# First stack of a two-stack kernel on one core: the norm factor moved from the rows to the projections, the transposes of x and y spread between the products

## The chip, the core and the metric

The kernel runs on one core of one Trainium2 chip. The metric is device time in microseconds, from the start of the program to its end; lower is better. All arithmetic is fp32 in and out; the products are made of fp32r pieces (below).

## The reference

A sequence of 256 rows of width 2048 goes through two stacks of two layers each. The change touches the first stack only. One of its layers is:

```python
h = rms_norm(x, norm_gain)                      # x * rsqrt(mean(x*x)+eps) * gain, per row
proj = jnp.einsum('bsd,de->bse', h, w_in)       # 2048 -> 10 segments of 2048
(da_q, da_k, da_v, da_z, sb_q, sb_k, sb_v, sb_z, gate_a, gate_b) = split_columns(proj)
...
q = rope(rms_norm(da_q..., qk_q_gain)); k = rope(rms_norm(da_k..., qk_k_gain))
oa = differential_attention(...);  ua = rms_norm(oa, subln_gain) * (1-lambda_init) * silu(da_z)
ub = stick_breaking_attention(sb_q, sb_k, sb_v) * silu(sb_z)
y = sigmoid(gate_a) * (ua @ w_branch_a) + sigmoid(gate_b) * (ub @ w_branch_b)
return x + y @ w_out
```

The second stack (convolution, windowed attention and a recurrent unit side by side) starts from the x that layer 1 of the first leaves.

## The kernel before, in words

**Products.** Every weight matrix is cut into *halves* of 128 x 1024 numbers (512 KB). SyncE loads them one after the other into a ring of four slots (`raw`, `RING = 4`). ScalarE rounds a half to `w_hi` (line 551), VectorE makes the rest `w_lo = raw - w_hi` (line 913), and with that the raw slot is free for the next load. TensorE multiplies each half with two stationary parts of the activations, `hT_hi` and `hT_lo`: `product` (lines 1431 to 1433) issues three matmuls of 128x512 for two row groups of two blocks of the half, so twelve matmuls for a half. Eight halves make a *unit* (512 output columns) in two banks of PSUM `acc`; units take turns between banks 0, 1 and 2, 3. ScalarE can only round half s when TensorE is through with half s-4 (`split_free`, `acc_ready`).

**A layer** of stack one has 52 units: 16 steps (8 heads of differential attention, "DA", then 8 of stick-breaking, "SB") of two units each, whose attention work is pushed in between the halves of the step that follows; 16 units of gates and branches (unit g0 = 32 onwards, groups j = 0 to 3 of four units); 4 units of output projection. Orders on all engines are written out by hand: `split(u, a, b)` on ScalarE and VectorE and `halves(u, stat, a, b)` on TensorE name the halves of unit u (numbers of 8 and more run on into the next unit) that are worked on before the next other piece. The layer loop is a hardware loop (`Fori`).

**Between stages.** TensorE needs activations with features on the partitions, so they are *turned* (transposed) by it, four transposes of 128x128 for two of the 16 feature chunks (a *group* f = 0 to 7) into PSUM `work[:, f % 4]`; ScalarE copies this to the hi part and VectorE makes the lo part. Three such places matter here:

- `layer_start` (TensorE line 1455): after all of x is loaded (layer 0), or after the last `add_x` (layer 1), ScalarE sums the squares of x (line 572), GpSimd raises the mean to the power -0.5 (line 383), VectorE scales the rows of x into `rows` (line 919), TensorE turns `rows` in 8 groups, ScalarE (580) and VectorE (935) fill `hT`. Only then does the first product of the layer start. The gain `kept[:, c]` is applied in 580 and 935.
- `turn_y` (TensorE line 1566): when the last branch unit is done, groups 0 to 5 are turned, then, after `branch(l, 3, 1)` on VectorE (lines 1038, 1041), groups 6 and 7; lines 673 and 1045 fill `hT` again, and the output projection starts.
- `add_x` (VectorE line 1052) adds each of the four output units to x.

A DA step starts on GpSimd with `rotate` (squares, norm and rotary part of q and k, lines 408 to 426), from the copy of the first unit (`evac_qk`, ScalarE line 594), and TensorE turns its result `QN` (line 1468) after the first half of the next step.

## Time and profile before

| | us |
|---|---|
| median of 3 runs (lowest, highest) | 3442.09 (3440.69, 3442.84) |
| the profiled execution: its own time | 3441.07 |
| its span in the trace | 3439.4 |
| TensorE busy | 3328.3 (97%) |
| VectorE, ScalarE, GpSimd busy | 1981.0, 1640.6, 502.1 |

Mean granted TensorE clock 0.987. The profile's span is 1.7 us shorter than the execution's own time, which in turn is 1.0 us under the median. Busy time of the pipelined matmuls overlaps, so a matmul's share of time is read from the distance between starts and not from its duration.

### The profile page before, as it was taken

The numbers are of one execution on the slowest core, as the hardware profiler recorded it, in microseconds if no ns is written. First come the engines' busy times: TensorE is split into PE (matmuls) and PEld (weight loads), VectorE is DVE, ScalarE is ACT, GpSimd is POOL, SyncE is SP. The second block draws the span as 40 slices with busy tenths as digits, with TensorE's granted clock in tenths as the row PEclk, the third lists the DMA queues.
The fourth block names the chain that finished last, engine by engine and source line by source line (L and its number), as shares of the span: only waits on it lengthen the run. The fifth ranks groups of instructions, "written<-read, shape, count | busy, mean of one in ns | idle before, by whom it ended". The sixth has DMA issues, their size and how long they took to land.

```text
span 3439.4 us, 49065 instructions
## 1 busy us (share of the span) xinstructions
PE 3328.3 (97%) x17528; PEld 2846.8 (83%) x17528; DVE 1981.0 (58%) x2194; ACT 1640.6 (48%) x2243; POOL 502.1 (15%) x426
## 2 busy tenths in 40 slices
PE   6999999999999989999999999999969999999998
PEld 5888888888888778888888888888769889898897
DVE  4667654545444456667544444444556775667765
ACT  4444455555444444454455554443434464544643
POOL 4444500000000015445300000000001000020000
PEclk9999999999999999999999999999989999999998
DMA  5455554455555445555545545555533334343342
GB/s 195 170 172 185 172 177 168 165 177 169 193 194 192 169 162 177 177 177 175 179 161 175 171 171 184 192 193 183 179 135 130 123 126 151 138 158 123 120 145 98
DMA packets 155021, 567.22 MB, mean 165 GB/s; under 512 B 17296, under 2 KB 17344, under 8 KB 154368
## 3 DMA queue, kind: packets, MB, share of 16 engines
q1 hardware_dynamic: 153216, 555.81, 47.3%
q0 software_dynamic: 1680, 9.67, 0.8%
q8 instruction: 86, 1.41, 0.2%
q14 instruction: 39, 0.32, 0.0%
HBM read 563.32 MB, written 2.10 MB: 164 GB/s over the span
## 4 chain that ended last, share of the span: by engine, by line
PE 94%; DVE 3%; ACT 1%; issue 1%; DMA 1%; POOL 0%; DVEq 0%; ACTq 0%; POOLq 0%
PE acc L1431 22%; PE acc L1433 22%; PE acc L1432 22%; PE acc L1642 6%; PE acc L1644 6%; PE acc L1643 6%; PE work L1468 1%; DVE w_lo L913 1%; PE work L1494 1%; PE work L1720 1%; PE work L1721 1%; PE work L1691 1%; PE work L1621 1%; PE work L1622 1%; PE work L1623 0%
## 5 line engine op out<-in xcount | busy, mean ns | idle before, releaser
L913 DVE TENSOR_TENSOR w_lo<-raw,w_hi 128x1024 fp32r<-128x1024 f32 x1056 | 1407.9, 1343 | 1200.1 <-ACT w_hi L551 929.5
L551 ACT ACTIVATE w_hi<-raw 128x1024 fp32r<-128x1024 f32 x832 | 876.5, 1059 | 980.4 <-PE acc L1433 977.0
L1431 PE MATMUL acc<-w_hi,hT_hi 128*128 128x512 f32 x2816 | 1115.4, 396 | 0.0
L1433 PE MATMUL acc<-w_hi,hT_lo 128*128 128x512 f32 x2816 | 1099.2, 390 | 0.0
L1432 PE MATMUL acc<-w_lo,hT_hi 128*128 128x512 f32 x2816 | 1097.2, 390 | 0.0
L1433 PEld LDWEIGHTS acc<-w_hi,hT_lo 128*128 128x128 f32 x2816 | 529.2, 188 | 113.0
L1432 PEld LDWEIGHTS acc<-w_lo,hT_hi 128*128 128x128 f32 x2816 | 530.3, 188 | 106.4
L1431 PEld LDWEIGHTS acc<-w_hi,hT_hi 128*128 128x128 f32 x2816 | 529.9, 188 | 105.1
L565 ACT ACTIVATE w_hi<-raw 128x1024 fp32r<-128x1024 f32 x224 | 236.1, 1056 | 396.0 <-PE acc L1644 382.8
L1642 PE MATMUL acc<-h_hi,w_hi 128*128 128x272 f32 x1152 | 344.7, 299 | 0.0
L1644 PE MATMUL acc<-h_hi,w_lo 128*128 128x272 f32 x1152 | 333.2, 289 | 0.0
L1643 PE MATMUL acc<-h_lo,w_hi 128*128 128x272 f32 x1152 | 331.5, 288 | 0.0
L1642 PEld LDWEIGHTS acc<-h_hi,w_hi 128*128 128x128 f32 x1152 | 216.8, 188 | 4.4 <-issue 2.4
L1643 PEld LDWEIGHTS acc<-h_lo,w_hi 128*128 128x128 f32 x1152 | 217.1, 188 | 1.5
L1644 PEld LDWEIGHTS acc<-h_hi,w_lo 128*128 128x128 f32 x1152 | 216.7, 188 | 0.0
L1642 PE MATMUL acc<-PJr,w_hi 128*128 128x272 f32 x512 | 150.7, 294 | 0.0
L1644 PE MATMUL acc<-PJr,w_lo 128*128 128x272 f32 x512 | 148.2, 289 | 0.0
L1643 PE MATMUL acc<-PJr,w_hi 128*128 128x272 f32 x512 | 147.4, 288 | 0.0
L377 POOL TENSOR_SCALAR ZG<-TZ 128x512 f32<-128x512 f32 x32 | 21.3, 664 | 718.6 <-ACT TZ L589 718.6
L319 DVE SCALAR_TENSOR_TENSOR PJ<-PJ,par 128x271 f32<-128x271 f32 (+14 forms) x240 | 106.6, 496 | 0.0
L1433 PE MATMUL acc<-w_hi,ubT_lo 128*128 128x512 f32 x256 | 99.6, 389 | 0.0
L1431 PE MATMUL acc<-w_hi,ubT_hi 128*128 128x512 f32 x256 | 99.6, 389 | 0.0
(314 smaller groups left out, 3598.9 us busy)
## 6 DMA issues: line engine op xcount, KB each, us to landing
raw<-weights SPq DMA_DIRECT2D x1056, 512.0 KB, 3.3
mat<-mats POOLq DMA_DIRECT2D x2, 1536.0 KB, 7.7
X<-x_in POOLq DMA_DIRECT2D x1, 2048.0 KB, 12.8
out<-out_rows SPq DMA_DIRECT2D x8, 256.0 KB, 2.3
par<-params POOLq DMA_DIRECT2D x2, 640.0 KB, 8.8
cst<-consts POOLq DMA_DIRECT2D x1, 872.0 KB, 5.8
cst<-consts POOLq DMA_DIRECT2D x1, 768.0 KB, 13.7
ropeC<-rope POOLq DMA_DIRECT2D x2, 256.0 KB, 8.8
```

The costliest lines, as they stand in the source:

```text
L319: return eng.scalar_tensor_tensor(o[:, j:TOK], x[:, 0:TOK - j], par2[:, w:w + 1], o[:, j:TOK], ALU.mult, ALU.add)
L551: act.activation(w_hi[:, slot, :], raw[:, slot, :], ACT.Copy).then_inc(hi_ready, 1)
L565: act.activation(w_hi[:, slot, :], raw[:, slot, :], ACT.Copy).then_inc(hi_ready, 1)
L913: dve.tensor_tensor(w_lo[:, s % RING, :], raw[:, s % RING, :], w_hi[:, s % RING, :], ALU.subtract)\
L1431: pe.matmul(o, stat[0][:, kc, token], hi, start=(kc == 0), stop=False)
L1432: pe.matmul(o, stat[0][:, kc, token], lo, start=False, stop=False)
L1433: ins = pe.matmul(o, stat[1][:, kc, token], hi, start=False, stop=(kc == KC - 1))
L1468: ins = pe.transpose(work[:, a // 2, o:o + P], src[:, t, a, :], ident)
L1494: pe.matmul(work[:, 2 + a, 0:384], cst[:, C_NEGTRI:C_NEGTRI + P], SM[:, a, :], start=False, stop=True, skip_group_check=True)
L1642: pe.matmul(o, hi, x_hi, start=(kc == 0), stop=False)
L1643: pe.matmul(o, hi, x_lo, start=False, stop=False)
L1644: ins = pe.matmul(o, lo, x_hi, start=False, stop=(kc == KC - 1))
```

## The change

1. **Norm factor.** x is no longer scaled before it is turned. `hT` holds x times gain, and the factor of each row (`rstdx`, or half of it for the gates' tanh) is the scale of the ScalarE copies that empty the projections: `evac_qk`, `evac_vz`, `evac_gate`. These become two instructions of 128x512 (one for each row group, since the scale is one number per partition) in place of one of 128x1024. The squares and the GpSimd chain move into the first step of the layer, before `evac_qk`.
2. **Layer 0.** x is loaded by SyncE in eight pieces of 256 columns (256 KB each, in runs of 1 KB), placed between the first four weight halves; the identity and the gains (`kept`, now of both layers) go with them. GpSimd's own loads wait until the eighth piece is there. TensorE turns groups 0 and 1, then a group after each of the first six halves.
3. **Layer 1.** x is turned during the output projection of layer 0: groups 0 to 5 within units 1 to 3, groups 6 and 7 after the second half of the new layer. The per-layer parameters are loaded when the last y is ready, not after the last `add_x`.
4. **y** is turned into `uaT`, which is no longer read then, in place of `hT`: groups 0 to 5 between halves 9 to 14 of the last branch unit pair, groups 6 and 7 after the first two halves of the output projection.
5. The layer loop is written out twice in place of a `Fori`, and some semaphores are merged.

```diff
         @block.sync
+            def x_part(f):
+                c = slice(256 * f, 256 * f + 256)
+                sp.dma_start(X[:, :, c], x_in[:, c].rearrange("(t p) n -> p t n", p=P)).then_inc(x_loaded[f], 16)
+            x_part(0)
+            sp.dma_start(cst[:, C_ID:C_ID + P], consts1[:, C_ID:C_ID + P]).then_inc(set_loaded, 16)
             for slot in range(RING):
                 sp.dma_start(raw[:, slot, :], weights[slot]).then_inc(raw_loaded[slot], 16)
+                if slot == 0:
+                    sp.dma_start(kept[:, :, :], kept1).then_inc(set_loaded, 16)
+                x_part(slot + 1)
+            for f in range(RING + 1, 8):
+                x_part(f)
...
         @block.scalar
             def layer_start(l):
-                act.wait_ge(x_loaded, 16)
-                act.wait_ge(x_added, 4 * l)
-                for t in range(NT):
-                    act.activation(rows[:, t, :], X[:, t, :], ACT.Square, accum_out=ssx[:, t:t + 1]).then_inc(x_ss, 1)
-                split(UNITS1 * l, 0, RING)
+                u = UNITS1 * l
+                if l == 0:
+                    act.wait_ge(set_loaded, 32)
+                    for f in range(8):
+                        split(u, f, f + 1)
+                        h_hi(l, f)
+                else:
+                    split(u, 0, 6)
+                    h_hi(l, 6)
+                    h_hi(l, 7)
+                    split(u, 6, 8)
+            def first_step(m):
+                split(u, 8, 10)
+                act.wait_ge(x_added, 4 * l)
+                for t in range(NT):
+                    act.activation(rows[:, t, :], X[:, t, :], ACT.Square, accum_out=ssx[:, t:t + 1]).then_inc(x_ss, 1)
+                split(u, 10, 12)
+                act.wait_ge(x_rstd, 2 * l + 2)
+                evac_qk(m)
+                split(u, 12, 14)
...
             def evac_qk(m):
-                act.activation(QK[...], acc[:, 0:2, :], ACT.Copy).then_inc(qk_evac, 1)
+                for t in range(NT):
+                    ins = act.activation(QK[:, t, :, :]..., acc[:, t, :], ACT.Copy, scale=rstdx[:, t:t + 1])
+                ins.then_inc(qk_evac, 1)
...
         @block.vector
             def layer_start(l):
-                dve.wait_ge(x_rstd, l + 1)
-                for t in range(NT):
-                    dve.tensor_scalar(rows[:, t, :], X[:, t, :], rstdx[:, t:t + 1], None, ALU.mult).then_inc(xn_ready, 1)
...
         @block.tensor
+            def turn_h(l, f):
+                if l:
+                    pe.wait_ge(x_added, 4 * (l - 1) + f // 2 + 1)
+                else:
+                    pe.wait_ge(x_loaded[f], 16)
+                if f >= 4:
+                    pe.wait_ge(hT_lo, 8 * l + (f - 3))
+                ... 4 transposes of X into work[:, f % 4] ...
+            def first_step(m):
+                if l == 0:
+                    pe.wait_ge(set_loaded, 32)
+                    turn_h(l, 0)
+                    turn_h(l, 1)
+                pe.wait_ge(qk_evac, m["n"])
+                for s in range(8):
+                    halves(u, hT, s, s + 1, (hT_lo, 8 * l))
+                    if l == 0 and s < 6:
+                        turn_h(l, s + 2)
+                    if l and s == 1:
+                        turn_h(l, 6)
+                        turn_h(l, 7)
...
                 pe.wait_ge(y_ready, 4 * l + 3)
+                halves(g0 + 14, ubT, 8, 9)
                 for f in range(6):
+                    halves(g0 + 14, ubT, 9 + f, 10 + f)
                     turn_y(l, f)
+                halves(g0 + 14, ubT, 15, 16)
+                halves(g0 + 16, uaT, 0, 2, out)
                 pe.wait_ge(y_ready, 4 * l + 4)
                 for f in (6, 7):
                     turn_y(l, f)
-                halves(g0 + 16, hT, 0, 8, (yT_lo, 8 * l))
...
+                for n in range(1, 4):
+                    halves(g0 + 16 + n - n % 2, uaT, 8 * (n % 2), 8 * (n % 2) + 2)
+                    for f in (2 * n - 2, 2 * n - 1):
+                        if l + 1 < DEPTH:
+                            turn_h(l + 1, f)
+                        halves(..., s, s + 1)
+                    halves(..., 8 * (n % 2) + 4, 8 * (n % 2) + 8)
```

Below is how this stands in the instruction order of TensorE at three places, with the semaphores that each instruction waits for. First the start of layer 0 before the change: all 32 transposes of `rows`, then the first half (its first three matmuls are shown).

```order
L1455 MATMUL work<-cst,rows 128x128 [waits xn_ready]
L1455 MATMUL work<-cst,rows 128x128 x15
...
L1455 MATMUL work<-cst,rows 128x128 [waits hT_lo]
L1455 MATMUL work<-cst,rows 128x128 x3
...
L1424 ISA [waits hT_lo,qk_evac]
L1431 MATMUL acc<-w_hi,hT_hi 128x512 [waits split_ready]
L1432 MATMUL acc<-w_lo,hT_hi 128x512
L1433 MATMUL acc<-w_hi,hT_lo 128x512
```

The same place with the change: eight transposes of `X`, the first half, and a group of four after it.

```order
L1532 MATMUL work<-cst,X 128x128 [waits x_loaded0,set_loaded]
L1532 MATMUL work<-cst,X 128x128 x3
L1532 MATMUL work<-cst,X 128x128 [waits x_loaded1]
L1532 MATMUL work<-cst,X 128x128 x3
L1506 MATMUL acc<-w_hi,hT_hi 128x512 [waits split_ready,hT_lo,qk_evac]
...
L1532 MATMUL work<-cst,X 128x128 [waits x_loaded2]
L1532 MATMUL work<-cst,X 128x128 x3
L1506 MATMUL acc<-w_hi,hT_hi 128x512 [waits split_ready,hT_lo]
```

The 24 transposes of groups 2 to 7 have moved from in front of the first half to places behind the first six halves. Next, the turning of y: before the change, behind the last half of the last branch unit (`ubT`), on TensorE.

```order
L1433 MATMUL acc<-w_hi,ubT_lo 128x512
...
L1566 MATMUL work<-cst,rows 128x128 [waits y_ready]
L1566 MATMUL work<-cst,rows 128x128 x15
...
L1566 MATMUL work<-cst,rows 128x128 [waits yT_lo,y_ready]
L1566 MATMUL work<-cst,rows 128x128 x3
...
L1431 MATMUL acc<-w_hi,hT_hi 128x512 [waits split_ready]
```

With the change, the rows around groups 5 to 7: group 5 stands between two halves of `ubT`, groups 6 and 7 behind two halves of the output projection (`uaT`).

```order
L1664 MATMUL work<-cst,rows 128x128 [waits yT_lo]
L1664 MATMUL work<-cst,rows 128x128 x3
L1506 MATMUL acc<-w_hi,ubT_hi 128x512 [waits split_ready]
...
L1508 MATMUL acc<-w_hi,uaT_lo 128x512
L1664 MATMUL work<-cst,rows 128x128 [waits yT_lo,y_ready]
L1664 MATMUL work<-cst,rows 128x128 x3
L1664 MATMUL work<-cst,rows 128x128 [waits yT_lo]
L1664 MATMUL work<-cst,rows 128x128 x3
L1506 MATMUL acc<-w_hi,uaT_hi 128x512 [waits split_ready,yT_lo]
```

What moved is the wait for the last y (`y_ready`): from between the transposes to behind two halves of the output projection. Last, TensorE at the start of layer 1 with the change (before, the rows there are those of the first block above, since the loop body is one).

```order
L1506 MATMUL acc<-w_hi,hT_hi 128x512 [waits split_ready,hT_lo,qk_evac]
...
L1508 MATMUL acc<-w_hi,hT_lo 128x512
L1532 MATMUL work<-cst,X 128x128 [waits hT_lo,x_added]
L1532 MATMUL work<-cst,X 128x128 x3
L1532 MATMUL work<-cst,X 128x128 [waits hT_lo,x_added]
L1532 MATMUL work<-cst,X 128x128 x3
L1506 MATMUL acc<-w_hi,hT_hi 128x512 [waits split_ready,hT_lo]
```

The layer's first two halves no longer stand behind any transpose; groups 6 and 7 follow them.

## Rows read from the trace of the kernel before

**Rows 1.** Waits of TensorE, longest first: us in total, times, longest.

```profile
PE work L1455 <- DVE rows L919: 33.3, 2, 24.3
...
PE work L1566 <- DVE rows L1041: 8.2, 2, 4.1
```

**Rows 2.** Timeline, layer 0's start, all engines: start, length, what, releaser.

```profile
0.87 1.82 SPq L352 DMA_DIRECT2D raw<-weights  x4
...
14.27 1.28 ACT L572 ACT_TABLE_LOAD   x1 [14.27 <-DMA X<-x_in]
15.57 1.91 ACT L572 ACTIVATE rows<-X 128x2048 f32<-128x2048 f32 x1
...
25.83 3.01 ACT L580 ACTIVATE hT_hi<-work,kept 128x256 fp32r<-128x256 f32 x8
...
30.54 6.34 DVE L935 SCALAR_TENSOR_TENSOR hT_lo<-work,kept,hT_hi 128x256 fp32r<-128x256 f32 x16
...
34.50 0.48 PE L1431 MATMUL acc<-w_hi,hT_hi 128*128 128x512 f32 x1
```

**Rows 3.** Timeline of TensorE around the turning of y, layer 0.

```profile
1162.09 3.27 PE L1566 MATMUL work<-cst,rows 128*128 128x128 f32 x24
1169.48 1.97 PE L1566 MATMUL work<-cst,rows 128*128 128x128 f32 x8 [4.12 <-DVE rows L1041]
1171.10 0.78 PE L1431 MATMUL acc<-w_hi,hT_hi 128*128 128x512 f32 x1
...
1174.50 0.39 PE L1433 MATMUL acc<-w_hi,hT_lo 128*128 128x512 f32 x1
```

**Rows 4.** One stretch: us, busy of PE, PEld, DVE, ACT, POOL, then PEclk, DMA.

```profile
1170.00:1174.50 4.50, 4.50 (x16) 3.77 (x14) 4.50 (x6) 1.19 (x2) 0.00 (x0) 0.53 0.58 189
```

**Rows 5.** Timeline of TensorE from layer 0's last product to layer 1's first.

```profile
1259.53 0.39 PE L1433 MATMUL acc<-w_hi,hT_lo 128*128 128x512 f32 x1
1268.94 3.68 PE L1455 MATMUL work<-cst,rows 128*128 128x128 f32 x16 [9.02 <-DVE rows L919]
...
1280.29 0.48 PE L1431 MATMUL acc<-w_hi,hT_hi 128*128 128x512 f32 x1
```

**Rows 6.** Timeline of TensorE, layer 1: four transposes (`turn_u`) inside a product.

```profile
2094.33 0.39 PE L1433 MATMUL acc<-w_hi,hT_lo 128*128 128x512 f32 x1
2094.56 0.60 PE L1523 MATMUL work<-cst,U 128*128 128x128 f32 x4
...
2097.54 0.39 PE L1433 MATMUL acc<-w_hi,hT_lo 128*128 128x512 f32 x1
```

**Rows 7.** Page, DMA queues (packets, MB, share) and issues (KB, us to landing).

```profile
q1 hardware_dynamic: 153216, 555.81, 47.3%
...
raw<-weights SPq DMA_DIRECT2D x1056, 512.0 KB, 3.3
...
out<-out_rows SPq DMA_DIRECT2D x8, 256.0 KB, 2.3
```

**Rows 8.** One stretch of the start; the last number is GB/s.

```profile
4.00:14.00 10.00, 0.00 (x0) 0.00 (x0) 0.00 (x0) 0.00 (x0) 1.06 (x3) 1.00 1.01 410
```

**Rows 9.** The first transfer of a weight half, issued at 0.9.

```profile
DMA to landing us min/median/max: 3.4/3.4/3.4
```

**Rows 10.** Timeline of ScalarE and VectorE at the end of output unit 0.

```profile
1238.25 1.06 ACT L551 ACTIVATE w_hi<-raw 128x1024 fp32r<-128x1024 f32 x1 [1.66 <-PE acc L1433]
1240.97 1.06 ACT L551 ACTIVATE w_hi<-raw 128x1024 fp32r<-128x1024 f32 x1 [1.66 <-PE acc L1433]
...
1239.35 1.23 DVE L913 TENSOR_TENSOR w_lo<-raw,w_hi 128x1024 fp32r<-128x1024 f32 x1 [1.50 <-ACT w_hi L551]
1240.49 1.22 DVE L1052 TENSOR_TENSOR X<-acc,X 128x1024 f32<-128x1024 f32 x1
```

**Rows 11.** Timeline, layer 0, second step: GpSimd, then TensorE.

```profile
77.70 2.76 POOL L426 TENSOR_TENSOR QN<-QN,small 128x1024 f32<-128x1024 f32 x1
...
80.86 1.04 PE L1468 MATMUL work<-cst,QN 128*128 128x128 f32 x8
```

More of the change, by code:

```diff
@@ L452, in step @@
                     rotate(this)
-            with pool.Fori(0, DEPTH) as l:
+            for l in range(DEPTH):
                 layer_start(l)
-                layer_steps(pool, l, step)
+                layer_steps(pool, l, rotate, step)
                 with pool.Fori(0, 4) as j:
@@ L1567, in turn_y, with gates @@
                 ins.then_inc(yT_turned, 1)
-            with pe.Fori(0, DEPTH) as l:
-                layer_start(l)
-                layer_steps(pe, l, step)
+            def gates(l, j):
+                g0 = UNITS1 * l + 2 * HEADS
+                pe.wait_ge(ya_ready, 4 * l + j)
+                halves(g0 + 4 * j, hT, 0, 8)
+                pe.wait_ge(yb_ready, 4 * l + j)
+                halves(g0 + 4 * j, hT, 8, 16)
+                branches(l, j)
+            for l in range(DEPTH):
+                layer_steps(pe, l, first_step, step)
                 g0 = UNITS1 * l + 2 * HEADS
```

265 lines of the change are left out of this document (158 added, 107 removed).

## The prediction

> **What bounds the kernel now.** I read the page first. TensorE is busy 97% of the span, so the question for any edit off TensorE is whether TensorE waits for it. The waits of TensorE [rows 1] say where it does in stack one: twice for the scaled rows at the start of a layer (33.3 us in all) and twice for the last y (8.2). Nothing else in stack one is in that list: the attention work between halves, the gates and the ring of weights hold nothing up. The timelines then give each of the four places its full price, which is more than the wait: transposes that stand alone, second waits, and a slow clock behind them.
>
> *Start of layer 0* [rows 2]. ScalarE waits 14.27 us for x, then come table load, squares, the GpSimd chain, the scaling, the transposes; the first product starts at 34.50. *Turning of y* [rows 3]. TensorE is through with the branches at 1162.09, the first product of the output projection starts at 1171.10. Its first eight matmuls take until 1174.50, 3.40 us, against 8 x 0.227 = 1.82 at the usual pace, for the granted clock is 0.53 in 1170 to 1174.5, so the 1.2 GHz level for nearly all of it [rows 4]; TensorE had stood idle 4.12 us just before. The place costs 9.01 + 1.58 = 10.6 us. Layer 1 shows the same. *From layer 0 to 1* [rows 5]. The last product ends at 1259.53 + 0.23 = 1259.76, the next starts at 1280.29: 20.5 us, with 0.1 for a slow first matmul 20.6.
>
> The usual pace comes from ScalarE's roundings, which are released half by half: 1238.25 and 1240.97, so 2.72 us for a half of twelve matmuls [rows 10].
>
> **The change part by part.**
>
> *What a group of four transposes costs inside the product stream.* The trace shows such groups in `turn_u`: from the matmul at 2094.33 to the twelfth after it at 2097.54 it takes 3.21 us with four transposes between, against 2.72 [rows 6]. So 0.49 us a group. The transposes stay; what goes is the emptiness around them. Eight groups cost 3.9 us.
>
> *y, twice.* 10.6 - 3.9 = 6.7 us each, 13.4 in all. Condition: the new waits are covered. The last y needs `branch(l, 3, 1)`, two VectorE instructions of the size of `add_x` (1.22 each [rows 10]), after the last branch half; TensorE has two halves (5.4 us) to do meanwhile. Per half VectorE has a split (1.23 [rows 10]) and the low part of a group (for y at most x's 0.8, below), ScalarE 1.06 and a hi part of about the same, against 3.2 us on TensorE. If that cover were gone, the old wait of 4.1 would be back.
>
> *Layer 0 to 1.* 20.6 - 3.9 = 16.7 us. Condition: `add_x` is done before the group that waits for it. Today a unit's last half ends just before 1238.25, and the add, behind one split on VectorE, ends at 1240.49 + 1.22 = 1241.7, 3.5 us later [rows 10]; the new order gives TensorE two halves first (5.4). So 1.9 us to spare, in each of units 1 to 3; before groups 6 and 7 the add stands behind no split. The parameter loads now run beside the weights, 1.1 MB against a ring with several us in hand; they used to fall into TensorE's wait.
>
> *Start of layer 0.* Here nothing in the trace shows the new order, so I build it. SyncE issues a transfer each 0.45 us from 0.87 on [rows 2]. The wires carry 410 GB/s from 4 to 14 us [rows 8]; the first half took 3.4 us and landed at 4.3 [rows 9]. Piece 0 and the identity (320 KB) add 0.8: first weight half at 5.2, `kept` at about 5.5. ScalarE: table load 1.28 [rows 2] to 6.5, rounding 1.06, hi part of a group 3.01/4 = 0.75; VectorE after the rounding 1.23, low part 6.34/8 = 0.8: the first product at 9.7. Until then groups 0 and 1 are turned. Then the slow clock: eight transposes after an idle stretch and then products is just the picture of [rows 3], so 1.6 us again (bounds 0 to 2.5). Six groups at 0.49 follow, 2.9. Against a start at 34.6 the stream stands as if it had begun at 9.8 + 1.6 + 2.9 = 14.3: 20.3 us won. Within a half and a group (3.2 us) ScalarE has 1.06 + 0.75 and VectorE 1.23 + 0.8, and from the end of a group to the half that needs it there are 2.7 us for 0.75 + 0.8. All SyncE transfers, 4.2 MB, are in by 14 at that rate, and weight half 4, asked for when half 0 is split (9), by 15.5; it is wanted at 24.
>
> *The factor on the copies.* Two copies of 128x512 in place of one of 128x1024 cost ScalarE some 0.1 us. In steps 1 and later GpSimd starts `rotate` only after ScalarE's squares of the head before, which wait for TensorE: nothing. In the first step of a layer nothing lies between. There `QN` is ready at 77.70 + 2.76 = 80.46 and TensorE wants it at 80.86, its weight load a little sooner [rows 11]: 0.2 to 0.4 us in hand. The squares, now ahead of `evac_qk`, hold ScalarE 2 x 1.91 = 3.8 us [rows 2]: after half 5 a split, the squares and two splits are 1.06 + 3.8 + 2 x 1.0 = 6.8 us, where two halves and a split give 5.44 + 1.06 = 6.5. In layer 1 `evac_qk` is so 0.3 late, in layer 0, where a group more lies between, not at all. I charge 0.3 us.
>
> *The loop written out, merged semaphores:* 0. The second stack is written out already and its products run at pace.
>
> Sum: 13.4 + 16.7 + 20.3 - 0.3 = 50.1 us. From the profiled execution's own 3441.07 (span 3439.4 and 1.7 around it): 3391.0. The median of the runs is 1.0 above it, so 3392.
>
> **A rule weighed.** Four weight halves are issued within 2 us [rows 2] and the wires then carry 410 GB/s without a break [rows 8]: cutting x into eight does not cost eight latencies. The Trainium skill (DMA: Bandwidth & Descriptors, "Anatomy of one DMA" and "Bandwidth") gives each DMA about 2.0 us fixed besides its bytes and advises at least 1 MiB in one. By adding that for the 14 first transfers the start would take about 38 us, as an estimate from that page, and the sum would lose nearly all of its 20.3; by the row it loses nothing.
>
> **The rivals.**
>
> *Pieces land one at a time.* If the first transfers followed each other at the pace of lone ones, 2.3 us for 256 KB and for the small ones, 3.3 for a half [rows 7], piece 7 would be in at 37, half 4 at 40, and half 7 of the first unit would end at 55.4, against 56.4 today. That takes 19.3 back: 3411. For it: nothing measured; against it: [rows 8].
>
> *Short runs are slow.* A piece of x has runs of 1 KB. The SyncE queue's packets, nearly all of 4 KB, took 47.3% x 16 x 3439 / 153216 = 0.17 us each [rows 7]. The lower bound of a 1 KB packet is a quarter of this, and that is in the sum. The upper bound is the same 0.17: then a piece takes 2.7 us, piece 7 is in at 32.4, half 4 at 34, and half 7 ends at 48, not 36: 12 back, 3404. I take the lower end, since nothing says that a packet costs by its number, but the truth may lie between.
>
> *The norm factor is late.* `evac_qk` of the first step waits for squares, GpSimd's tables and pow. Layer 0 is the likelier place, as GpSimd's loads (1.9 MB) start only after piece 7. At half of 410 GB/s they take 9 us and are in by 24, squares are done at 35; so they must be over twice as slow before it costs. From there on each us late is a us of TensorE at the first `QN`; with 2 to 8 us of it, 3394 to 3400.
>
> *Slower than before.* 24 groups (6 at the start, 6 and 6 for y, 6 for x) now stand between halves, and ScalarE and VectorE do their copies in line with the splits. If each such group made TensorE wait because the split behind a copy came late, by 50.1 / 24 = 2.1 us a group or more, the kernel would be slower. VectorE has 2.0 us of work in 3.2, so this needs an order in which one engine waits for another in each round. I followed the order and found none.
>
> *The change does not do it:* were x or y still waited for at the old places, 3442. The order excludes it.
>
> **How the numbers follow.** My forecast 68% (3387 to 3396), short runs in part or whole 13% (3396 to 3405), late factor 8% (3393 to 3400), pieces one at a time 4% (3405 to 3412), slower 2%; 5% for a start or clocks better than that (under 3387). The range 3386 to 3402 leaves out about 2 in 10. A difference of 0.2%, 7 us, is about what can be told from no change: faster 0.96, same 0.02, slower 0.02.
>
> **What will show it.** First product near 9.7, the second unit's first half (half 8) near 36; no wait of TensorE on lines of `turn_y` or `turn_h` over 1 us; pace 0.227 on both sides of the last branch half and of the layer border; granted clock 1.00 there; `QN` without a wait. I am wrong if x pieces or weight half 4 land late, if TensorE waits for `x_added`, or if a step in the middle of stack one is longer than it was.

## The result, and the profile after

| | before | changed |
|---|---|---|
| median of 4 runs (lowest, highest), us | 3442.02 (3440.69, 3442.84) | 3393.49 (3391.20, 3394.28) |
| the profiled execution: own time, span, us | 3441.07, 3439.4 | 3391.20, 3389.4 |
| mean granted TensorE clock | 0.987 | 0.992 |

The ratio of the medians is 0.9858, with a 95% interval of 0.9844 to 0.9871: 48.5 us faster. The forecast was 3392.0 with a range of 3386 to 3402. The profiled execution is the quickest of the four; the spans of the other three are 2.1 to 3.1 us longer; these have no trace, and what may vary from run to run comes up at the end.

TensorE's share on the page of the changed kernel, the row that answers to the 97% of before:

```profile
PE 3319.6 (98%) x17528; PEld 2838.2 (84%) x17528; DVE 1966.8 (58%) x2190; ACT 1653.5 (49%) x2322; POOL 498.9 (15%) x425
```

The waits of TensorE in the changed kernel (us in total, times, longest) that lie in stack one; the others belong to stack two:

```profile
PE work L1532 <- DMA kept<-kept: 5.8, 1, 5.8
...
PE acc L1506 <- DVE hT_lo L971: 2.3, 1, 2.3
...
PE work L1566 <- POOL QN L440: 1.0, 1, 1.0
```

The two rows of [rows 1] are gone, 41.5 us of idle time in four places; 9.1 us in three places are left, and all three lie in the first 63 us. [rows 1] leaves out a third row of stack one, and the prediction's sentence that nothing else of it is in the list is wrong:

```profile
PE work L1455 <- DVE hT_lo L935: 8.3, 2, 4.6
```

It is the second wait at the two layer starts. The prediction's prices hold all the same, since they were taken from the timelines, from end to start; with it the waits of before are 49.8 us. In the changed kernel line 1532 is the transposing of x, 1506 to 1508 the products, 1566 the turning of `QN`. There is no row for y (line 1664) and none for `x_added`.

The timeline of the start of the changed kernel (start, length, what, what ended the idle time before), to be read beside [rows 2]:

```profile
1.75 0.42 SPq L359 DMA_DIRECT2D raw<-weights  x1
...
5.60 1.28 ACT L565 ACT_TABLE_LOAD   x1 [5.60 <-DMA raw<-weights]
...
5.76 2.13 PE L1532 MATMUL work<-cst,X 128*128 128x128 f32 x8 [5.76 <-DMA kept<-kept]
...
10.17 0.76 PE L1506 MATMUL acc<-w_hi,hT_hi 128*128 128x512 f32 x1 [2.28 <-DVE hT_lo L971]
10.74 0.63 PE L1507 MATMUL acc<-w_lo,hT_hi 128*128 128x512 f32 x1
11.16 0.63 PE L1508 MATMUL acc<-w_hi,hT_lo 128*128 128x512 f32 x1
...
15.20 0.60 PE L1532 MATMUL work<-cst,X 128*128 128x128 f32 x4
...
17.73 0.77 POOL L383 DMA_DIRECT2D cst<-consts  x1 [17.29 <-DMA X<-x_in]
...
34.47 1.91 ACT L607 ACTIVATE rows<-X 128x2048 f32<-128x2048 f32 x1
...
40.69 1.26 ACT L630 ACTIVATE QK<-acc,small 128x512 f32<-128x512 f32 x2 [0.43 <-POOL small L390]
...
62.75 1.09 PE L1566 MATMUL work<-cst,QN 128*128 128x128 f32 x8 [1.00 <-POOL QN L440]
```

Four things are to be seen. The first product starts at 10.17 (34.50 before). Its first half lasts until 15.20, 5.03 us in place of 2.72, with matmuls 0.43 us apart. GpSimd's wait for the eighth piece of x ends at 17.73. The first turning of `QN` comes at 62.75, against 80.86 before [rows 11], and TensorE has waited 1.00 us for it. That wait is the last row: it is small, but before the change TensorE never waited there. The two ScalarE rows above it, the first of the squares of x and the copy of q and k (`evac_qk`), are taken up in the account of the prediction.

The same view around the last y and at the border of the layers, for [rows 3] and [rows 5]:

```profile
1143.23 0.60 PE L1664 MATMUL work<-cst,rows 128*128 128x128 f32 x4
...
1147.87 1.22 DVE L1109 TENSOR_TENSOR rows<-rows,yB 128x1024 f32<-128x1024 f32 x1
...
1151.86 1.03 PE L1664 MATMUL work<-cst,rows 128*128 128x128 f32 x8
...
1194.31 1.22 DVE L1120 TENSOR_TENSOR X<-acc,X 128x1024 f32<-128x1024 f32 x1
...
1197.26 0.60 PE L1532 MATMUL work<-cst,X 128*128 128x128 f32 x4
...
1242.71 1.03 PE L1532 MATMUL work<-cst,X 128*128 128x128 f32 x8
...
1255.73 1.91 ACT L607 ACTIVATE rows<-X 128x2048 f32<-128x2048 f32 x1
```

The last y is done at 1147.87 + 1.22 = 1149.09 and is wanted at 1151.86, 2.8 us later. The first `add_x` is done at 1195.53 and its group stands at 1197.26, 1.7 us later. None of the TensorE rows has a bracket: it waited for nothing. The windows of the two stretches and of the start (us, busy of PE, PEld, DVE, ACT, POOL, then PEclk, DMA share, GB/s), for [rows 4] and [rows 8]:

```profile
3.00:17.00 14.00, 8.96 (x30) 6.93 (x31) 5.49 (x8) 7.08 (x11) 0.00 (x0) 1.00 0.98 336
...
10.00:14.50 4.50, 4.33 (x10) 3.46 (x11) 3.25 (x5) 1.77 (x3) 0.00 (x0) 1.00 1.03 371
...
1140.00:1156.00 16.00, 16.00 (x80) 13.36 (x79) 10.92 (x12) 7.50 (x10) 1.70 (x3) 1.00 0.61 219
1230.00:1250.00 20.00, 20.00 (x94) 16.62 (x93) 11.30 (x12) 8.92 (x12) 0.00 (x0) 1.00 0.55 184
```

Around y and around the border TensorE is busy for the whole stretch at a granted clock of 1.00, where [rows 4] has 0.53. At the start the loads run at 336 GB/s, less than the 410 of [rows 8]; and the clock of 1.00 there does not fit the slow matmuls of the timeline (see the last section).

**Where the 50.0 us of span come from.** The first turning of `QN` in each layer and the last run of the same instruction, in the layer's last step (there it turns `QK`), are good landmarks, since they are the same instruction in both kernels. They stand at 80.86, 810.74, 1326.63 and 2056.5 before and at 62.75, 792.29, 1284.43 and 2013.95 after, and the last `add_x` of the stack at 2505.76 and 2456.22:

| stretch | predicted | measured |
|---|---|---|
| start of layer 0 (to the first `QN`) | 20.3 | 18.1 |
| 15 steps of layer 0 | 0 | 0.3 |
| y and the border of the layers | 6.7 + 16.7 - 0.3 = 23.1 | 23.75 |
| 15 steps of layer 1 | 0 | 0.35 |
| y of layer 1 | 6.7 | 7.0 |
| stack two | 0 | 0.5 |
| sum | 50.1 | 50.0 |

The sum is nearly exact because an error of 2.2 at the start is made good by five small terms of the other sign. That is luck. So the experiments ask two things: whether each part is worth what its term says, and what the 2.2 us are.

### The profile page after: what moved, and what is told of

Read it like the earlier page. It is cut to its first block, busy times and chain, and to the rows that moved or that the text cites. A ratio compares the mean times of both kernels' runs of the same rounds, so it can differ in the third digit from the quotient of the medians.

```text
span 3389.4 us, 48369 instructions
## 1 busy us (share of the span) xinstructions
PE 3319.6 (98%) x17528; PEld 2838.2 (84%) x17528; DVE 1966.8 (58%) x2190; ACT 1653.5 (49%) x2322; POOL 498.9 (15%) x425
## 4 chain that ended last, share of the span: by engine, by line
PE 95%; DVE 3%; ACT 1%; POOL 1%; issue 0%; DMA 0%; SPq 0%; ACTq 0%; DVEq 0%; POOLq 0%
PE acc L1506 22%; PE acc L1508 22%; PE acc L1507 22%; PE acc L1757 6%; PE acc L1759 6%; PE acc L1758 6%; PE work L1566 1%; DVE w_lo L965 1%; PE work L1592 1%; PE work L1835 1%; PE work L1836 1%; PE work L1806 1%; PE work L1736 1%; PE work L1737 1%; PE work L1738 1%
## 5 line engine op out<-in xcount | busy, mean ns | idle before, releaser
L1506 PE MATMUL acc<-w_hi,hT_hi 128*128 128x512 f32 x2560 | 1015.2, 397 | 2.3 <-DVE hT_lo L971 2.3
L1508 PE MATMUL acc<-w_hi,hT_lo 128*128 128x512 f32 x2560 | 998.9, 390 | 0.0
L1507 PE MATMUL acc<-w_lo,hT_hi 128*128 128x512 f32 x2560 | 997.5, 390 | 0.0
L1508 PEld LDWEIGHTS acc<-w_hi,hT_lo 128*128 128x128 f32 x2560 | 481.0, 188 | 102.7
L1506 PEld LDWEIGHTS acc<-w_hi,hT_hi 128*128 128x128 f32 x2560 | 481.5, 188 | 97.8 <-issue 2.7
L1507 PEld LDWEIGHTS acc<-w_lo,hT_hi 128*128 128x128 f32 x2560 | 481.8, 188 | 95.8
L1506 PE MATMUL acc<-w_hi,uaT_hi 128*128 128x512 f32 x512 | 199.9, 391 | 0.0
L1508 PE MATMUL acc<-w_hi,uaT_lo 128*128 128x512 f32 x512 | 199.3, 389 | 0.0
L1507 PE MATMUL acc<-w_lo,uaT_hi 128*128 128x512 f32 x512 | 199.2, 389 | 0.0
L390 POOL TENSOR_SCALAR ZG<-TZ 128x512 f32<-128x512 f32 x32 | 34.3, 1072 | 721.6 <-ACT TZ L624 721.6
```

The costliest lines, as they stand in the source:

```text
L390: return pool.tensor_scalar(*operands)
L1506: pe.matmul(o, stat[0][:, kc, token], hi, start=(kc == 0), stop=False)
L1507: pe.matmul(o, stat[0][:, kc, token], lo, start=False, stop=False)
L1508: ins = pe.matmul(o, stat[1][:, kc, token], hi, start=False, stop=(kc == KC - 1))
```

## The experiments

Each kernel starts from the changed one and computes the reference in full unless the text says otherwise. "The changed kernel" has 3393.49 below. All were compared with fresh runs of the kernel before on the same chip (3441.70, 3442.01 and 3441.42 in the three sets); the changed kernel itself was not run again in them. Two kernels whose edits should save nothing, or less than 1 us, come out 1.8 and 1.7 us under it, so a difference of under 2 us from 3393.49 says nothing by itself, and is read from the rows.

### The norm factor alone

y, x of layer 1 and x of layer 0 are turned in front of the products again, and x comes in one transfer; only the norm factor on the projections is kept. The edits at y and at layer 1 are those of the next two experiments; the diff shows those of layer 0, without the orders of ScalarE and VectorE, which follow (four splits, then the eight groups).

```diff
                 if l == 0:
                     pe.wait_ge(set_loaded, 32)
-                    turn_h(l, 0)
-                    turn_h(l, 1)
+                for f in range(8):
+                    turn_h(l, f)
...
-            x_part(0)
+            sp.dma_start(X[:, :, :], x_in.rearrange("(t p) n -> p t n", p=P)).then_inc(x_loaded[0], 16)
...
-                x_part(slot + 1)
-            for f in range(RING + 1, 8):
-                x_part(f)
```

> Against the changed kernel (3393.5): x comes in one transfer, all eight groups are turned ahead of the first product of both layers, and y is turned behind the last branch half as before. Only the norm factor stays on the projections. My terms: y +13.4; layer 1's start +4.5, since without squares, pow and scaling the first product can follow the last add_x by about 8.4 us instead of 20.6; layer 0's start +4.7. So 3416, and the norm factor alone is worth about 26 of the 48.5 us. Rival: the factor is worth little and the spreading of the transposes does the work; then 3430 or more.

Measured: 3415.94 (3412.17 to 3417.00), ratio to before 0.9925 [0.9909, 0.9942]. Two of its waits, and the row that ends GpSimd's wait for x:

```profile
PE work L1523 <- DMA kept<-kept: 9.9, 1, 9.9
...
PE work L1650 <- DVE rows L1104: 8.3, 2, 4.2
```

```profile
9.13 0.77 POOL L380 DMA_DIRECT2D cst<-consts  x1 [8.69 <-DMA X<-x_in]
```

The wait for y (8.3, twice) is that of before. The wait for `QN` is not among the rows. So of the 48.5 us this kernel has 26, and the other 22.5 come from hiding the transposes and from the pieces. But the 26 are not the norm factor's alone, for this kernel keeps the new order of the loads as well: x, `kept` and the identity stand in SyncE's queue and x ahead of the weights. So x is there at 9.13 and TensorE starts to turn it at 9.92, where before the change ScalarE waited for it until 14.27 [rows 2]. By these rows some 4.4 us of the gain at the start belong to the loads, and some 22 us in all to taking squares, power and scaling out of the chain before the transposes. That is an estimate from 14.27, 9.92 and 26; no kernel with the factor moved and the old loads was run. The landmarks of the profiled executions divide it further: of the gain of this kernel 13.0 us lie at the start (of 18.1) and 13.7 at the border; what it lacks against the changed kernel is 5.1 at the start, 10.0 from y of layer 0 and the border, and some 6 at y of layer 1.

### y turned at the old place

```diff
-                halves(g0 + 14, ubT, 8, 9)
-                for f in range(6):
-                    halves(g0 + 14, ubT, 9 + f, 10 + f)
-                    turn_y(l, f)
-                halves(g0 + 14, ubT, 15, 16)
+                halves(g0 + 14, ubT, 8, 16)
+                for f in range(6):
+                    turn_y(l, f)
...
-                halves(g0 + 16, uaT, 0, 2, out)
                 pe.wait_ge(y_ready, 4 * l + 4)
...
-                halves(g0 + 16, uaT, 2, 8, out)
+                halves(g0 + 16, uaT, 0, 8, out)
```

ScalarE and VectorE have their copies of y behind the splits again, to match.

> The changed kernel with y turned behind the last branch half again (still into uaT). By my term 2 x 6.7 us come back: 3407, with the idle wait of 4.1 us, and the granted clock at the 1.2 GHz level for some 3 us behind it, in both layers. Rival: part of the old cost was the write into hT, that is the buffer; then less than 5 us come back.

Measured: 3409.25 (3406.03 to 3409.57), ratio 0.9905 [0.9889, 0.9922], so 15.8 us by the medians. By the landmarks of the profiled execution the stretch with the first y, from the last landmark of layer 0 to the first of layer 1, is 6.3 us longer (498.40 against 492.14) and the one with the second 6.9 (449.16 against 442.27); the rest is a start that was 1.36 us later by chance. The timeline of this kernel:

```profile
1145.01 3.27 PE L1662 MATMUL work<-cst,rows 128*128 128x128 f32 x24
1152.45 1.56 PE L1662 MATMUL work<-cst,rows 128*128 128x128 f32 x8 [4.17 <-DVE rows L1108]
1153.66 0.78 PE L1504 MATMUL acc<-w_hi,uaT_hi 128*128 128x512 f32 x1
1154.23 0.63 PE L1505 MATMUL acc<-w_lo,uaT_hi 128*128 128x512 f32 x1
```

The picture of [rows 3] is back: 4.17 us idle, then matmuls 0.43 apart, at a granted clock of 0.50 from 1153 to 1156 us. The term of 6.7 each stands. The rival, that the write into `hT` was the cost, is excluded: this kernel writes into `uaT`, and all of it came back.

### x of layer 1 turned in front of the layer

```diff
                     turn_h(l, 1)
+                else:
+                    for f in range(8):
+                        turn_h(l, f)
...
-                    if l and s == 1:
-                        turn_h(l, 6)
-                        turn_h(l, 7)
...
-                        if l + 1 < DEPTH:
-                            turn_h(l + 1, f)
```

> The changed kernel with layer 1's x turned in eight groups after the last add_x and ahead of the layer's first product; the norm factor stays on the projections. My theory: squares, pow and scaling were 12 of the 16.7 us of this place, so only about 4.5 come back: 3398. Rival: turning within the output projection carries the whole gain: 3410.

Measured: 3399.15 (3398.23 to 3400.39), ratio 0.9875 [0.9859, 0.9892]: 5.7 us. TensorE at the border of this kernel:

```profile
1237.03 1.91 PE L1526 MATMUL work<-cst,X 128*128 128x128 f32 x16
1240.55 0.63 PE L1526 MATMUL work<-cst,X 128*128 128x128 f32 x4 [1.60 <-DVE hT_lo L968]
...
1243.73 0.78 PE L1500 MATMUL acc<-w_hi,hT_hi 128*128 128x512 f32 x1
```

From the end of the products to the first one of layer 1 it is 1243.73 - 1237.03 = 6.7 us, of which 3.9 were for the transposes anyway. By the landmarks the border is 3.5 us longer, some 0.5 of it a slow clock behind 1243.73. So 3.5 of the border's gain belong to the hiding and 13.7 to the norm factor; with 6.3 for y that makes 23.5 of the 23.75. The remaining 2.2 us by the medians are not fully placed. Part may lie in the steps: this execution waited for `QN` four times, 2.9 us in all, where the changed kernel did once. I come back to this.

### Every turned group twice

In all places each group of x and y is transposed twice into the same place, so that each costs TensorE double. The output is that of the reference; half of the transposes are useless. The diff is that of x; y has the same.

```diff
+                        pe.transpose(work[:, f % 4, o:o + P], X[:, t, c * P:c * P + P], ident)
+                for c in (2 * f, 2 * f + 1):
+                    for t in range(NT):
+                        o = c % 2 * SEQ + t * P
                         ins = pe.transpose(work[:, f % 4, o:o + P], X[:, t, c * P:c * P + P], ident)
```

> The changed kernel with every group of four transposes of x and y issued twice in a row, 32 more groups. My theory: TensorE pays for each group what it takes in its own stream, 0.49 us for the first and some 0.4 for a second behind it, and the copies hide behind the products: + 13 us, 3406. Rival (the one in which groups hold up the chain of copies and splits): a group's cost is mostly waiting, then under 5 us, or it grows beyond 20 because the spare time of the copies is used up.

Measured: 3407.99 (3406.42 to 3410.52), ratio 0.9902 [0.9886, 0.9919]. For the 16 groups (8 of y, 8 of x) of the stretch from the last landmark of layer 0 to the first of layer 1 the landmarks give 6.95 us, 0.43 each: a group costs TensorE's own time for it, and no more. That excludes the slower rival, by which a group would hold up the splits. From the first product to the first `QN`, with six doubled groups, it is 52.96 us against 52.58, only 0.4 more, and the timeline of this kernel says why:

```profile
6.81 1.12 PE L1532 MATMUL work<-cst,X 128*128 128x128 f32 x4 [6.81 <-DMA kept<-kept]
...
11.22 0.47 PE L1506 MATMUL acc<-w_hi,hT_hi 128*128 128x512 f32 x1 [0.74 <-DVE hT_lo L971]
11.54 0.39 PE L1507 MATMUL acc<-w_lo,hT_hi 128*128 128x512 f32 x1
11.76 0.39 PE L1508 MATMUL acc<-w_hi,hT_lo 128*128 128x512 f32 x1
```

With 16 transposes and 0.74 us idle in front of it, the first half runs at full pace, 0.227 apart, from its first matmul. It pays the extra groups with the slow half that it saves.

### TensorE kept busy before the first product

This tests the clock directly. Matmuls on zeros, whose results nothing reads, fill TensorE's two empty stretches at the start. VectorE sets the tile `U` to zero first (`junk_set`).

```diff
+                    pe.wait_ge(junk_set, 1)
+                    for _ in range(5):
+                        pe.matmul(work[:, 3, 0:256], U[:, 0, 0:P], U[:, 0, :], start=True, stop=True)
                     pe.wait_ge(set_loaded, 32)
                     turn_h(l, 0)
                     turn_h(l, 1)
+                    for _ in range(6):
+                        pe.matmul(work[:, 3, 0:256], U[:, 0, 0:P], U[:, 0, :], start=True, stop=True)
```

> The changed kernel, with TensorE kept busy at the start by eleven matmuls on a zeroed tile whose result nobody reads: five before the first transposes, six between them and the first product. My theory: the first half took 5.0 us in place of 2.7 only because the clock stood at its 1.2 GHz level after an idle stretch; so the first product starts at the same time and its matmuls come 0.23 us apart and not 0.43: 2.3 us less, 3391. Rival: the slow first half is due to the transfers that then run at full rate beside it; then its matmuls stay 0.43 apart.

Measured: 3390.80 (3389.72 to 3391.71), ratio 0.9851 [0.9834, 0.9867], 2.7 us under the changed kernel. Its first half:

```profile
10.75 0.47 PE L1508 MATMUL acc<-w_hi,hT_hi 128*128 128x512 f32 x1 [0.47 <-issue]
13.56 0.60 PE L1534 MATMUL work<-cst,X 128*128 128x128 f32 x4
```

2.81 us from the first product to the group, in place of 5.03. From the first product to the first `QN` it is 50.39 us against 52.58. So the slow clock costs 2.2 us here, and is removed by useless work alone. The rival, the transfers that run beside it, is excluded: they are the same here. The first product starts at 10.75, not at the same time as expected, because the first weight half landed later (6.17 against 5.60).

### x in one transfer

```diff
-            x_part(0)
+            sp.dma_start(X[:, :, :], x_in.rearrange("(t p) n -> p t n", p=P)).then_inc(x_loaded[0], 16)
...
-                x_part(slot + 1)
-            for f in range(RING + 1, 8):
-                x_part(f)
...
```

> The changed kernel with x in one transfer of 2 MB on SyncE's queue ahead of the weights, nothing else moved. By the rate of 410 GB/s, x lands near 7.7 us and the first weight half near 9 in place of 5.5, so the first product starts 3.5 us later and all is 3 to 3.5 slower: 3397. By the rule on fixed costs (pieces cost some 2 us each) it is faster than the eight pieces, below 3390.

Measured: 3395.04 (3394.11 to 3396.06), ratio 0.9862 [0.9846, 0.9879], 1.6 us over the changed kernel. Timeline and window of this kernel:

```profile
9.95 1.28 ACT L562 ACT_TABLE_LOAD   x1 [9.95 <-DMA raw<-weights]
...
14.53 0.76 PE L1503 MATMUL acc<-w_hi,hT_hi 128*128 128x512 f32 x1 [2.46 <-DVE hT_lo L968]
```

```profile
3.00:17.00 14.00, 4.44 (x14) 3.59 (x15) 4.59 (x7) 5.69 (x8) 2.43 (x5) 1.00 1.01 408
```

In the same stretch the pieces have 336 GB/s. The 408 include GpSimd's own loads, which start here at 9.32; from 3 to 8 us, where SyncE's queue is alone in both kernels, the rates are 396 and 286. But the first weight half stands behind 2 MB, and the first product is 4.4 us later. A fixed time of 2 us for each of the eight pieces, one after the other, would have made the pieces the slower way; they are the faster one. The Trainium skill (DMA: Bandwidth & Descriptors, "Bandwidth") advises at least 1 MiB in one DMA for most of the peak rate; the trace agrees about the rate (396 against 286), and the time goes by what lands first. That advice of the Trainium skill (same section) rests on transfers issued by GpSimd, and the pieces are SyncE's. Between the profiled executions 3.9 us of this reach the end of the span (3393.3 against 3389.4); by the medians it is 1.6, with ranges that touch. The profiled execution of the changed kernel was its quickest, with the earliest first product of all kernels with pieces but the last one; still, `QN` is first turned at 66.86 here and at 64.18 in the latest of the kernels with pieces.

### x in runs of 2 KB

The input is laid out so that a piece of x is one block with 2 KB for each partition, in place of two runs of 1 KB.

```diff
-                sp.dma_start(X[:, :, c], x_in[:, c].rearrange("(t p) n -> p t n", p=P)).then_inc(x_loaded[f], 16)
+                sp.dma_start(X[:, :, c], x_in[f]).then_inc(x_loaded[f], 16)
```

> The changed kernel with x laid out in memory so that a piece is one run of 2 KB for each partition and not two of 1 KB; all else the same. My theory: the short runs made the first 17 us run at 336 GB/s where it was 410 in the kernel before, so piece 7 is in by 15 to 16 in place of 17.2 to 17.7; and since nothing waits for it, the time stays 3393. Rival: the run length has no part in it, and piece 7 lands as before; or the first product moves too, by more than 0.5 us.

Measured: 3391.71 (3390.37 to 3392.76), ratio 0.9851 [0.9835, 0.9868]. The traffic from 3 to 17 us in this kernel:

```profile
DMA packets 3040, 4.68 MB, mean 335 GB/s; under 512 B 358, under 2 KB 2394, under 8 KB 3040
```

335 GB/s, as with 1 KB (336), and GpSimd's wait for piece 7 ends at 17.17, not at 15 to 16; in the other kernels with pieces it ends at 17.10 to 17.89. Most packets are still under 2 KB, probably because the destination, two row blocks of X, is still cut in 1 KB. So the first theory is refuted, and this shows only that the length of the runs in the source is not what holds the rate; whether longer packets would lift it is open. The median is 1.8 us under that of the changed kernel although the profiled start is later (first product at 11.43), and the ranges overlap.

### The cover of the last y taken away

Groups 6 and 7 of y follow the branch units directly; nothing is put in between.

```diff
                 halves(g0 + 14, ubT, 15, 16)
...
-                halves(g0 + 16, uaT, 0, 2, out)
                 pe.wait_ge(y_ready, 4 * l + 4)
                 for f in (6, 7):
                     turn_y(l, f)
-                halves(g0 + 16, uaT, 2, 8, out)
+                halves(g0 + 16, uaT, 0, 8, out)
```

> The changed kernel with groups 6 and 7 of y directly behind the last branch half, so that the two halves of the output projection no longer cover the two VectorE instructions of the last y. My theory: TensorE waits for these, about 2.6 us in each layer, and the clock keeps its level over so short a wait: + 5.2, 3399. Rival: any wait of this kind drops the clock, and 1.5 us more go in each layer: 3402.

Measured: 3397.84 (3397.08 to 3399.90), ratio 0.9872 [0.9856, 0.9889]: 4.35 us for two places, 2.2 each. By the landmarks it is 2.8 in each layer (494.97 against 492.14, and 445.10 against 442.27); that is the better number, for the medians carry the spread of the starts. Timeline and window:

```profile
1148.88 1.06 PE L1664 MATMUL work<-cst,rows 128*128 128x128 f32 x8 [2.62 <-issue]
1149.70 0.47 PE L1506 MATMUL acc<-w_hi,uaT_hi 128*128 128x512 f32 x1
```

```profile
1146.00:1150.00 4.00, 1.38 (x11) 1.13 (x10) 3.68 (x4) 1.06 (x1) 0.92 (x2) 1.00 0.44 131
```

TensorE stands idle 2.62 us and the clock stays at 1.00; the next product runs at full pace. The row names no releaser, but what stands ahead of the group is `branch(l, 3, 1)`, two VectorE instructions of 1.22. So the prediction's "the old wait of 4.1 would be back" was too dear: with groups 0 to 5 already in their places, the wait is 2.6, and no slow clock follows. Of the 6.3 to 6.9 us at each y, 2.8 belong to the two halves of cover; the rest goes, by difference, to the six groups that went between halves earlier and to the clock.

### The first copy no longer waits for the second power

```diff
-                act.wait_ge(x_rstd, 2 * l + 2)
+                act.wait_ge(x_rstd, 2 * l + 1)
                 evac_qk(m)
+                act.wait_ge(x_rstd, 2 * l + 2)
                 split(u, 12, 14)
```

`evac_qk` uses the factor itself and not its half, which GpSimd makes after it.

> The changed kernel with one wait moved: the first copy of q and k waits for the norm factor alone and not for its half too, which only the gates need. My theory: the wait of 1.0 us for the first QN in layer 0 comes from the lateness of that copy (squares, then GpSimd), 0.43 us of which is this wait; so the wait shrinks by 0.4 to 0.9 us, and nothing else moves: 3393, not told from the changed kernel by time, but by the row. Rival: GpSimd's own chain is longer by a step of 1.15 us in that place, then the wait stays 1.0 or grows by whole steps.

Measured: 3391.75 (3389.67 to 3393.72), ratio 0.9855 [0.9840, 0.9870]. The wait that it is about, in this kernel:

```profile
63.48 1.09 PE L1567 MATMUL work<-cst,QN 128*128 128x128 f32 x8 [0.87 <-POOL QN L440]
```

0.87 in place of 1.00. From the first product to the copy it is 30.25 us against 30.52, so the copy does start 0.3 earlier; GpSimd's chain then takes 0.4 longer (21.0 against 20.6) and eats it. The median cannot be told from the changed kernel's. The half of the factor is not the reason of the late copy.

### A better version

Useless matmuls as above (five and four), ScalarE's table load with a small instruction before its first wait, `kept` issued before the first weight half, the squares of x after halves 6 and 7 of layer 0, and the shorter wait of the experiment before.

```diff
+                    act.wait_ge(junk_set, 1)
+                    act.activation(small[:, 80:81], U[:, 0, 0:1], ACT.Copy)
                     act.wait_ge(set_loaded, 32)
                     for f in range(8):
                         split(u, f, f + 1)
...
+                        if f >= 6:
+                            square_x(f - 6)
                         h_hi(l, f)
...
             sp.dma_start(cst[:, C_ID:C_ID + P], consts1[:, C_ID:C_ID + P]).then_inc(set_loaded, 16)
+            sp.dma_start(kept[:, :, :], kept1).then_inc(set_loaded, 16)
...
```

> The changed kernel with four small edits at the start: the table load of ScalarE ahead of the first weights, the gains loaded ahead of the first weight half, TensorE kept busy with matmuls on zeros (5 and 4), the squares of x of layer 0 between the copies of groups 6 and 7 in place of behind half 9, and the wait of the run before this one. By my theory 1.3 (table) + 2.3 (clock) + 1.0 (wait for QN) us come off: 3389. Rival: these are hidden behind the landing of the first weight half, then less than 2 us come off.

Measured: 3387.48 (3386.98 to 3388.61, 5 runs), ratio 0.9844 [0.9830, 0.9857]. It is 6.0 us under the changed kernel, and its highest time is below the lowest of that; the medians of 1.7 and 1.8 us under 3393.49 above say that part of the 6.0 may be spread. By the profiled executions `QN` is first turned 3.6 us earlier (59.20 against 62.75). Timeline:

```profile
0.73 1.28 ACT L595 ACT_TABLE_LOAD   x1 [0.73 <-PEq L2170]
...
6.59 1.06 ACT L565 ACTIVATE w_hi<-raw 128x1024 fp32r<-128x1024 f32 x1 [4.36 <-issue]
...
9.88 0.47 PE L1519 MATMUL acc<-w_hi,hT_hi 128*128 128x512 f32 x1
12.70 0.60 PE L1545 MATMUL work<-cst,X 128*128 128x128 f32 x4
...
59.20 1.03 PE L1584 MATMUL work<-cst,QN 128*128 128x128 f32 x8
```

The table load is out of the chain, the first half takes 2.82 us, and `QN` has no bracket: the wait of 1.00 is gone. From the first product to `QN` it is 49.32 us, 1.07 less than in the kernel with the useless matmuls alone. The copy starts 26.78 us after the first product, against 30.52; 2.2 of this are the clock, 1.5 the squares. What is left is the landing of the first weight half, here at 6.6.

## Why the prediction was right, and where a term was off

**What bounds.** Right, but for the row of 8.3 us that the list of waits had and the sentence on it denied. All that stack one gained lies in the four places named; the steps between them changed by 0.3 us in fifteen.

**The cost of a group.** Predicted 0.49 from [rows 6]. In the changed kernel a half with a group takes 3.19 us (from 1143.23 back to 1140.04) against 2.72, and doubled groups cost 0.43 each. Right.

**y.** Predicted 6.7 each. Putting it back cost 6.3 and 6.9. Right, and the conditions too: 2.8 us to spare before the last y. One sentence in it was wrong, the price of taking the cover away (4.1 predicted; the wait is 2.6 and the landmarks give 2.8).

**The border.** 23.75 with the first y, predicted 23.1. The order's slack for `add_x` was 1.7 us, predicted 1.9. The 0.3 us for a late factor in layer 1 did not come: `QN` had no wait there. What I had not divided is whose gain it is: 13.7 us come from the norm factor, 3.5 from the hidden transposes and 6.3 from y.

**Start of layer 0: the mechanism was right, the size off, 20.3 predicted and 18.1 measured.** The terms, one by one:

- First product at 9.7 predicted, 10.17 measured, and 10.46 to 11.53 in the other kernels with pieces and without a change at this place. The first weight half landed at 5.6, not 5.2, though it was issued at 1.75: 3.8 us in place of the 3.4 of [rows 9]. This landing varies: 0.5.
- Slow clock 1.6 predicted, 2.3 measured. In [rows 3] eight matmuls were slow, here eleven. The useless matmuls gave back 2.2 of it. I had taken the size from the other place, within my bounds of 0 to 2.5.
- Six groups 2.9, measured 2.9 (15.20 to 31.20 in five rounds of 3.20).
- The wait for `QN` 0 predicted, 1.0 measured. This is the step that failed: the order "in layer 0, where a group more lies between, not at all". I took the group between as time won, since it holds TensorE. It costs ScalarE more. In layer 0 half 5 ends at 31.20; then ScalarE copies group 7 (31.84) and only then does both splits, of halves 8 and 9, so that the squares start at 34.47, 3.27 us after half 5. In layer 1 the split of half 8 is done by then and no copy comes: half 5 ends at 1254.51 and the squares start at 1255.73, 1.22 us after it. From the squares to the copy of q and k both layers take 6.22 us, of which the last 0.43 is a wait for GpSimd's powers, which I had not counted either. So the copy stands 22.48 us ahead of the first turning of `QN` in layer 1, where 0.39 are to spare, and would stand 21.06 ahead of it in layer 0 if TensorE did not wait: 1.4 us too few, 0.4 to spare, 1.0 of wait. The better version moves the squares ahead of this crowd, and the wait is gone.

0.5 + 0.7 + 1.0 = 2.2 us.

**The loads.** 410 GB/s taken over, 336 measured; piece 7 at 17.7, not at 14. It cost nothing, since it is wanted only after half 5, at 31.20. The rival "short runs are slow" may be right in part of its fact, since the rate is lower, and is wrong in its price; why the rate is lower stays open, for the experiment with 2 KB in the source does not find the reason. "Pieces land one at a time" is excluded by 17.7 (37 by that rival), "the norm factor is late" came in with 1.0 us and not with 2 to 8, and "slower" by the price of a doubled group.

## What to carry to other kernels

A factor per row can be taken out of the chain ahead of a product and put on the copy behind it; by estimate that gave some 22 us of 48.5 here, the new order of the loads some 4.4, and the hidden transposes and the pieces the other 22.5. Work of an engine that is hidden between products costs its own length and no more as long as the wait in front of it has two halves of cover: count the chain over all engines up to the consumer: a copy that is hidden from TensorE still holds up what stands behind it on ScalarE, and GpSimd's small instructions count too. At the start of a program, load first what the first product needs, in small pieces, put table loads ahead of the waits, and fill TensorE's gap with anything.

## What the runs showed of the hardware

**The clock at the start is not in its record.** In 10 to 14.5 us the granted clock of the changed kernel reads 1.00 (the 2.4 GHz level), while its matmuls start 0.427 us apart, as they do after the gap in the kernel with y at the old place, where the record reads 0.50 (1.2 GHz). That useless matmuls or more transposes bring back 0.227 says that it was the lower level. The first entry of the clock in the trace of the changed kernel stands at 14.9, just where its matmuls become quick; in the kernel with doubled groups it stands at 11.2, at the first product. A window ahead of the first entry reads 1.00 because nothing is recorded there. The Trainium skill (TensorE: Matmul & The Clock Gate, "Wait — 56ns, not 53.3ns?") gives 426.7 ns from start to start for a matmul of 512 columns at 1.2 GHz, and the row agrees. The distance of starts is the safer witness. The clock stayed up over 2.62 us of idle time after a long busy stretch, and was down after 4.12 and 4.17. But the length of the gap does not decide alone: at the border the kernel with x of layer 1 turned late and the one with the norm factor alone have the same gap of 1.60 us among the same transposes, and the clock is 0.50 behind it in the first (1241.5 to 1244.5) and 1.00 in the second (1250 to 1254). At the start 2.28 us of idle time after eight transposes left it low, and 16 transposes (with 0.74 us idle after them) brought it up.

**GpSimd and VectorE hold each other up, and who waits changes.** GpSimd's chain from the squares of q and k to `QN` takes 19.6 us in nearly all steps, and `QN` is then ready 0.5 us before TensorE turns it; in some steps it takes 20.75, and TensorE waits 0.64. Two such steps of the kernel with x of layer 1 turned late, one 48 us after the other, GpSimd and VectorE:

```profile
144.58 3.45 DVE L962 TENSOR_TENSOR w_lo<-raw,w_hi 128x1024 fp32r<-128x1024 f32 x2
...
145.63 1.32 POOL L432 TENSOR_TENSOR QN<-QK,ropeC 128x512 f32<-128x512 f32 x1
...
192.54 2.35 DVE L962 TENSOR_TENSOR w_lo<-raw,w_hi 128x1024 fp32r<-128x1024 f32 x2
...
193.59 2.45 POOL L432 TENSOR_TENSOR QN<-QK,ropeC 128x512 f32<-128x512 f32 x1
```

In the first, GpSimd takes 1.32 and VectorE 3.45 for its two; in the second, the same instructions take 2.45 and 2.35. The 1.1 us has changed sides. Both instructions read two operands from on-chip memory (SBUF). The Trainium skill (GPSIMD Engine Reference, "Key points") names contention of GpSimd with VectorE instructions that have two SBUF inputs, and these rows agree. Apart from the first step of a layer, where the chain is 20.5 to 21.8 in every kernel, the profiled executions had none of the longer steps, except this one (three) and the one with doubled groups (five, 3.3 us). Part of the spread between runs may come from it. What starts it was not tried.

**The first landing varies.** The first weight half, issued at 1.75 to 2.22, has landed at 5.60 in the changed kernel and at up to 6.96 in the others with pieces, and the first product moves with it, from 10.17 to 11.53. So a single pair of executions can't settle a question of 1 us here.
